# Head norms of two query stages: squares in two rounded halves, a new order on ScalarE and VectorE

## The chip, the cores and the metric

One core of a Trainium2 chip runs the whole kernel in one launch. The metric is the device time of that launch in microseconds; each kernel is executed several times, and the median counts. The core's engines run in parallel, each its own list in order, and wait for each other on semaphores: TensorE (PE: matmuls into PSUM), VectorE (DVE), ScalarE (ACT), GpSimd (POOL), and SyncE (SP), which here issues the DMAs.

## The reference

A transformer block (pooling mixer, windowed attention, convolutional FFN) is followed by two blocks with joint context: grouped-query attention, called l0, and latent attention, called l1, over 1024 tokens of width 1024 and 256 context tokens. What matters here is how queries and keys are made: project, norm each head of 64, rotate.

```python
def rms_norm(x, w):
    xf = x.astype(jnp.float32)
    y = xf * lax.rsqrt(jnp.mean(xf * xf, axis=-1, keepdims=True) + NORM_EPS)
    return (y * w.astype(jnp.float32)).astype(x.dtype)
...
    # first block
    q = partial_rope(rmsnorm(q, q_norm[l]), positions) * scale
    k = partial_rope(rmsnorm(k, k_norm[l]), positions)
...
    # second block
    k, v, q, g = jnp.split(h @ p["w_in"], cuts, axis=-1)
    q = apply_axial_rope(rms_norm(q.reshape(B, S, GQA_KV_HEADS, GQA_GROUP_2, GQA_HEAD_DIM), p["q_norm"]), cos, sin)
    k = apply_axial_rope(rms_norm(k.reshape(B, S, GQA_KV_HEADS, GQA_HEAD_DIM), p["k_norm"]), cos, sin)
```

## The kernel before

Activations lie transposed: features on the 128 partitions, tokens along the free axis. Every projection is made in split precision. Weights and inputs are each stored as a high part, rounded to fp32r, and a low part, the rounding's remainder; `split3` (L279) issues hi*hi, hi*lo and lo*hi into one PSUM bank. Weights come in panels of 128 output features by 1024: the SP queue loads a panel to `w_stage` (`load_next`, L200), ScalarE rounds it to `w_hi` (`next_hi`, L236, the instruction at L227), VectorE subtracts to `w_lo` (`next_lo`, L244, at L233). Two panel buffers alternate.

The stages in question are the first block's queries (stream q, 8 panels), and the second's queries (stream l0_q, 8 panels) and keys (stream l0_k, 2 panels). One **unit** is one panel, two heads, times one chunk of tokens. The first block has chunks of 512 and 512 (`CHUNKS_X`); l0 has 512, 512 and 256 (`CHUNKS_ALL`), called A, B and C here. That gives 16, 24 and 6 units. The work of a unit u:

- TensorE: 24 projection matmuls (8 steps of `split3`) into a bank; the stages use 4 banks, in l0 3, in turn. Then `pe_mean` (L895) of the unit **before**: the squares times a block matrix of ones, which sums them over each head. It is a plain fp32 matmul; the profile shows it as two rows of one line, L898. So the order is products(u+1), mean(u), products(u+2), mean(u+1), and at the end of a stage mean of the last but one and mean of the last unit follow each other directly (`lagged`, L917).
- ScalarE: `act_raw` (L829): Square of the bank to `heads_sq` (L833), then the bank times the gain to `heads_zg` (L834), which also sets the bank free. After the mean, `act_scale` (L859): Ln and Exp(-0.5 x) give the reciprocal root `heads_rs` (L862, L864). Its order is scale(u), raw(u+1).
- VectorE: `dve_finish` (L866): zg times cos (L882), shuffle (L884), times sin (L885), add (L886), times rs (L888), then a cast to fp32r, the high part of the query (`heads_qh`, L891), and a subtraction for the low part (`heads_ql`, L892).
- SP: stores both parts to DRAM (L910, L911).

The order of all this is written by hand, in loops that each engine runs for itself (`heads_pe`, `heads_act`, `heads_dve`, `heads_sp`); two panels make one loop body. At a stage's end the other engines wait for each other and for the stores (`end_phase`, L173), but TensorE goes on with the next stage's products as far as weights and free banks allow. Behind the keys comes the value stage (`l0_v`), whose banks are cleared by ScalarE and VectorE once they have left the key stage. The first block's keys (`kv1_*`) use the same helper class with their own calls, as do the heads of l1.

Of the kernel before, what the change touches and what calls it, by code (L numbers as in the profile page):

```python
# [104 lines left out]
def mixed_program(nc, A, out):  # L105

    ctx = ExitStack()
    with ctx:

        def sem(name):  # L110
            return ctx.enter_context(nc.semaphore(name))
# [4 lines left out]
        class Scope:  # L116


            def __init__(self):
                self.stack = ExitStack()  # L120
# [679 lines left out]
        class HeadBuffers:  # L800
            def __init__(self, name, scope):
                def two(what, dt=F32):
                    return [scope.sb(f"{name}_{what}{b}", [P, C], dt) for b in range(2)]
                self.ZG, self.SQ, self.RS = two("zg"), two("sq"), two("rs")
# [4 lines left out]
        heads_before = [0, 0]  # L809

        class Heads:

# [2 lines left out]

            def __init__(self, units, bufs, rows, dim, gain, sums, tables, mask, evacuated=None):
# [6 lines left out]
                self.j0, self.l0 = heads_before  # L825
                heads_before[0] += units
                heads_before[1] += units * self.links

# [64 lines left out]
                   .then_inc(self.split, 1)  # L893

            def pe_mean(self, pe, j, b, n):  # L895
                pe.wait_ge(self.sq, j + (self.j0 + 1))
                r = self.rows
                pe.matmul(SIDE[b][0:r, 0:n], self.sums.bitcast(F32), self.b.SQ[b][0:r, 0:n], start=True, stop=True)\  # L898
                  .then_inc(self.mean, 1)

            def begin(self, dve):
# [11 lines left out]
        def body_units(st, chunks, per_panel=1):  # L913

            return [(s, m, c, o, n) for s in range(2) for m in range(per_panel) for c, (o, n) in enumerate(chunks)]
# [14 lines left out]
                        finish(i, u - 1)  # L930
            pairs(eng, st.panels // 2, body)

        def heads_act(act, hd, st, chunks, banks, per_panel=1):
            act.preload_act_table_set(LN_EXP)
            units = body_units(st, chunks, per_panel)
            U = len(units)

            def begin(i, u):
                n = units[u][4]
                act.wait_ge(units_done, i * U + (st.u0 + u + 1))  # L940
                hd.act_raw(act, i * U + u, u % 2, BANK[u % banks][0:hd.rows, 0:n], n)


            lagged(act, st, U, begin, lambda i, u: hd.act_scale(act, i * U + u, u % 2, units[u][4]), finish_first=True,
                   after=lambda i, last, s: next_hi(act, st, i, last, s))

        def heads_dve(dve, hd, st, chunks, per_panel=1):
            units = body_units(st, chunks, per_panel)
            U = len(units)
            hd.begin(dve)  # L950

            def body(i, last):
                for u in range(U):
                    if (u + 1) % (U // 2) == 0:
                        next_lo(dve, st, i, last, 2 * u // U)
                    hd.dve_finish(dve, i * U + (EVAC_CREDIT + st.u0 + u + 1), i * U + u, u % 2, units[u][3], units[u][4],
                                  i * (U // 2) + u // 2)
            pairs(dve, st.panels // 2, body)

        def heads_pe(pe, hd, st, chunks, banks, HH, HL, kt=KT, per_panel=1, width=P, ready=None):  # L960
# [89 lines left out]
        heads_q1 = Heads(16, hb1, P, 64, vec("q_gain"), blocks[:, :], (COS1, SIN1), MASK1)  # L1050
# [1182 lines left out]
        tmp = Scope()  # L2233
        hb0 = HeadBuffers("heads0", tmp)
        MASK_GQA = [r ^ 16 for r in range(32)]
        heads_q0 = Heads(24, hb0, P, 64, vec("l0_q_gain"), blocks[:, :], TAB0, MASK_GQA)
        heads_k0 = Heads(6, hb0, P, 64, vec("l0_k_gain"), blocks[:, :], TAB0, MASK_GQA)
        tmp.close()
        tmp = Scope()
        values0 = Values("l0v", tmp, 256)  # L2240
# [1002 lines left out]
```

## Time and profile before

| what | value |
|---|---|
| median of 3 executions | 3487.97 us (3487.5 to 3494.04) |
| the profiled execution | 3487.57 us, span of its trace 3485.8 us |
| TensorE busy, share of the span | 3358.7 us, 96% |
| VectorE, ScalarE, GpSimd busy | 64%, 51%, 43% |
| first query stage in the trace | about 153 to 260 us |
| second query stage | about 1548 to 1678 us |
| keys of l0 | about 1678 to 1712 us |

The page of the profile gives busy time by engine, a chain of work that ended last (followed back from the last instruction through whatever released each), and groups of instructions. The trace below it is read by stretches of time. A row "[1.62 <-ACT heads_sq L833]" says that the engine stood idle for 1.62 us before this instruction, until that one had ended. Ends of matmuls are modelled: consecutive matmuls overlap in the rows, and the distance of their starts is what they cost.

### The profile page before, as it was taken

Reading aid. Unit: us, or ns where it says so; the run is one execution under the profiler, and the core shown is the slowest. Engines: PE = TensorE matmul, PEld = TensorE weight load, DVE = VectorE, ACT = ScalarE, POOL = GpSimd, SP = SyncE. Lnnn points to the kernel's source line nnn. Section 1 sums busy time; section 2 is a strip of 40 time slices with the busy share of each in tenths; the row PEclk is TensorE's granted clock in tenths of the full one; section 3 lists DMA queues with packets and bytes.
Section 4 is the critical chain, followed back from the end, with each engine's and each line's share of the span. In section 5 each row is a group of like instructions: output and inputs, shape, how many; then the busy total and the mean of one; then the engine's idle time right before and its main releaser. Section 6 shows DMA issues by size and latency. Waiting matters only on the chain.

```text
span 3485.8 us, 48222 instructions
## 1 busy us (share of the span) xinstructions
PE 3358.7 (96%) x15124; PEld 2675.2 (77%) x15124; DVE 2247.7 (64%) x2664; ACT 1768.6 (51%) x3036; POOL 1506.3 (43%) x952
## 2 busy tenths in 40 slices
PE   7999999999999999999999999999998999999999
PEld 5777878778888888778877777768675668888877
DVE  6674878577576665648627777767548875555551
ACT  3342868332010100234329999971455658888880
POOL 3402444444444444310037777757220026666652
PEclk9999999999999999999999999999999999999999
DMA  2134232411212121123344344323245344233312
GB/s 102 49 117 127 61 82 55 151 49 56 89 47 93 53 79 64 43 78 111 119 129 92 75 105 98 84 68 111 100 182 161 129 128 120 61 80 68 69 43 72
DMA packets 196086, 313.53 MB, mean 90 GB/s; under 512 B 100928, under 2 KB 111680, under 8 KB 195968
## 3 DMA queue, kind: packets, MB, share of 16 engines
q1 hardware_dynamic: 195968, 312.01, 31.1%
q8 instruction: 68, 1.11, 0.1%
q14 instruction: 50, 0.41, 0.0%
HBM read 234.02 MB, written 77.92 MB: 89 GB/s over the span
## 4 chain that ended last, share of the span: by engine, by line
PE 65%; POOL 10%; issue 10%; DVE 9%; ACT 4%; DMA 1%; SPq 0%; ACTq 0%; POOLq 0%; DVEq 0%
PE PBX L281 10%; PE PBX L283 10%; PE PBX L282 10%; POOL gqa_pl L2156 8%; PE PMX L281 5%; PE PMX L282 5%; PE PMX L283 5%; PE PD L2072 2%; PE PMX L2027 2%; PE PD L2073 2%; PE PD L2074 2%; PE PBX L2054 2%; PE PD L898 2%; PE PBX L2053 2%; PE PBX L2055 2%
## 5 line engine op out<-in xcount | busy, mean ns | idle before, releaser
L216 POOL TENSOR_TENSOR w_hi<-w_stage,zero 128x1024 fp32r<-128x1024 f32 (+2 forms) x123 | 227.2, 1847 | 1280.3 <-PE PBX L283 783.6
L2156 POOL TENSOR_TENSOR gqa_pl<-gqa_pf,gqa_ph 128x512 fp32r<-128x512 f32 (+1 forms) x288 | 381.7, 1342 | 138.4 <-ACT gqa_ph L2115 136.7
L2156 POOL TENSOR_TENSOR mla_pl<-mla_pf,mla_ph 128x512 fp32r<-128x512 f32 x256 | 341.2, 1338 | 190.3 <-ACT mla_ph L2115 184.8
L218 POOL TENSOR_TENSOR w_lo<-w_stage,w_hi 128x1024 fp32r<-128x1024 f32 (+2 forms) x123 | 300.4, 2442 | 9.6
L2178 DVE TENSOR_REDUCE mla_m<-PMX 128x1 f32<-128x1280 f32 x126 | 187.9, 1492 | 172.5 <-PE PMX L2027 172.5
L2178 DVE TENSOR_REDUCE gqa_m<-PMX 128x1 f32<-128x1280 f32 (+1 forms) x142 | 198.6, 1398 | 153.4 <-PE PMX L2027 152.7
L1720 ACT ACTIVATE conv_in<-PBX 128x512 f32<-128x512 f32 x66 | 39.5, 599 | 480.6 <-PE PBX L283 476.7
L2109 ACT ACTIVATE mla_pf<-PBX 128x512 f32<-128x512 f32 x320 | 190.2, 594 | 75.4 <-PE PBX L2055 61.1
L2115 ACT ACTIVATE gqa_ph<-gqa_pf 128x512 fp32r<-128x512 f32 (+1 forms) x352 | 215.0, 611 | 12.1
L2109 ACT ACTIVATE gqa_pf<-PBX 128x512 f32<-128x512 f32 (+1 forms) x352 | 200.6, 570 | 26.4 <-PE PBX L2058 20.3
L281 PE MATMUL PBX<-ffn_hi,w_hi 128*128 128x512 f32 x528 | 206.8, 392 | 3.8 <-DVE ffn_lo L672 3.8
L2115 ACT ACTIVATE mla_ph<-mla_pf 128x512 fp32r<-128x512 f32 x320 | 201.8, 631 | 11.4
L283 PE MATMUL PBX<-ffn_hi,w_lo 128*128 128x512 f32 x528 | 205.5, 389 | 0.0
L282 PE MATMUL PBX<-ffn_lo,w_hi 128*128 128x512 f32 x528 | 205.5, 389 | 0.0
L1747 DVE SCALAR_TENSOR_TENSOR conv_out<-conv_in,VEC,conv_out 128x1024 f32<-128x1024 f32 x88 | 187.0, 2125 | 12.8 <-DVE conv_out L1747 0.6
L281 PE MATMUL PBX<-l_hi,w_hi 128*128 128x512 f32 (+1 forms) x408 | 159.1, 390 | 8.1 <-DVE l_lo L672 6.2
L1743 DVE TENSOR_SCALAR conv_out<-conv_in,VEC 128x1024 f32<-128x1024 f32 x44 | 71.7, 1630 | 137.4 <-ACT conv_in L1720 137.2
L451 DVE SCALAR_TENSOR_TENSOR PMX<-mod_w,cond_s 128x1024 f32<-128x1024 f32 x96 | 151.8, 1581 | 5.7 <-DVE PMX L451 0.6
L1482 POOL TENSOR_TENSOR swa_pl<-swa_pf,swa_ph 128x512 fp32r<-128x512 f32 x64 | 81.2, 1269 | 158.9 <-ACT swa_ph L1426 158.6
L283 PE MATMUL PBX<-l_hi,w_lo 128*128 128x512 f32 (+1 forms) x408 | 146.3, 359 | 0.0
L282 PE MATMUL PBX<-l_lo,w_hi 128*128 128x512 f32 (+1 forms) x408 | 146.1, 358 | 0.0
L281 PE MATMUL PBX<-h_hi,w_hi 128*128 128x512 f32 x336 | 139.7, 416 | 6.6 <-POOL w_lo L1468 5.4
(430 smaller groups left out, 9966.2 us busy)
## 6 DMA issues: line engine op xcount, KB each, us to landing
mod_w<-in_w_mod SPq DMA_DIRECT2D x48, 512.0 KB, 3.5
w_stage<-in_w_up SPq DMA_DIRECT2D x44, 512.0 KB, 3.5
w_stage<-in_w_go SPq DMA_DIRECT2D x24, 512.0 KB, 3.6
gqa_k<-kh_d SPq DMA_DIRECT2D x32, 320.0 KB, 4.8
gqa_q<-qh_d SPq DMA_DIRECT2D x32, 320.0 KB, 6.9
w_stage<-in_w_down SPq DMA_DIRECT2D x24, 384.0 KB, 3.1
qh_d<-heads_qh SPq DMA_DIRECT2D x32, 256.0 KB, 2.1
ql_d<-heads_ql SPq DMA_DIRECT2D x32, 256.0 KB, 2.3
```

The costliest lines, as they stand in the source:

```text
L216: pool.tensor_tensor(w_hi[s][:, 0:st.cols], w_stage[s][:, 0:st.cols], z, ALU.add).then_inc(w_hi_done, 1)
L218: pool.tensor_tensor(w_lo[s][:, 0:st.cols], w_stage[s][:, 0:st.cols], w_hi[s][:, 0:st.cols].bitcast(F32), ALU.subtract).then_inc(w_split, 1)
L281: pe.matmul(ps, wh, xh, start=first, stop=False)
L282: pe.matmul(ps, wh, xl, start=False, stop=False)
L283: return pe.matmul(ps, wl, xh, start=False, stop=last)
L451: dve.scalar_tensor_tensor(out=PMX[:, C:3 * C], in0=bufs[s], scalar=1.0, in1=conds[j], op0=ALU.mult, op1=ALU.mult, accum_out=MOD[:, bass.d ...
L1482: pool.tensor_tensor(swa_PL[K % 4][:, :, 0:m], swa_PF[K % 2][:, :, 0:m], swa_PH[K % 4][:, :, 0:m].bitcast(F32), ALU.subtract).then_inc(a1[ ...
L1747: dve.scalar_tensor_tensor(out=y, in0=CU[s][:, j:j + S], scalar=w(j), in1=y, op0=ALU.mult, op1=ALU.add).then_inc(conv_step, 1)
L2109: act.activation(self.PF[k % 4][:, 0:n], self.S[k % 2][:, 0:n], ACT.Exp, scale=self.scale)\
L2115: act.activation(self.PH[k % 4][:, 0:n], self.PF[k % 4][:, 0:n], ACT.Copy).then_inc(self.hi, 1)
L2156: eng.tensor_tensor(self.PL[k % 4][:, 0:n], self.PF[k % 4][:, 0:n], self.PH[k % 4][:, 0:n].bitcast(F32), ALU.subtract).then_inc(self.lo_dv ...
L2178: dve.tensor_reduce(self.M[g % 2][:, t:t + n], MX[:, 0:n * w].rearrange("p (n w) -> p n w", n=n), AX.X, ALU.max, negate=True).then_inc(sel ...
```

## The change

A second way to norm heads is added, used by all three stages named above (`heads_act`, `heads_dve` and `heads_pe` now issue only it). The mean is made of two fp32r matmuls in place of one fp32 matmul, and its input of two parts: ScalarE rounds the squares to a high half, VectorE subtracts to a low half. The query's high part is rounded by ScalarE in place of VectorE. VectorE works in the order rotate(u), times rs(u), [w_lo], low part(u), cos(u+1), low half of the squares(u+1); ScalarE in the order scale(u), Square(u+1), query high(u), zg(u+1), squares high(u+1), [w_hi]. The mean of a unit now waits for VectorE's low half of the squares. The new buffers `sq_low` and `sq_high` lie on the same memory as `sq` and `rs`.

```diff
+            def act_begin(self, act, j, b, ps, n):
+                act.wait_ge(self.split, j + (self.j0 + 1))
+                act.activation(self.b.SQ[b][:, 0:n], ps, ACT.Square).then_inc(self.sq, 1)
+            def act_halves(self, act, j, b, ps, n):
+                act.activation(self.b.ZG[b][:, 0:n], ps, ACT.Copy, scale=self.gain).then_inc(self.evacuated, 1)
+                act.wait_ge(self.sq, j * 2 + (self.s0 + 1))
+                act.activation(self.b.RSR[b][:, 0:n], self.b.SQ[b][:, 0:n], ACT.Copy).then_inc(self.sq, 1)
+            def act_high(self, act, j, b, n, pair):
+                act.wait_ge(self.link, j * self.links + (self.l0 + 5))
+                act.wait_ge(self.stored[b], pair * 32 + (16 * self.j0 + 32))
+                act.activation(self.b.QH[b][:, 0:n], self.b.T1[:, 0:n], ACT.Copy).then_inc(self.link, 1)
+            def dve_squares_low(self, dve, j, b, n):
+                dve.wait_ge(self.sq, j * 2 + (self.s0 + 2))
+                sq = self.b.SQ[b][:, 0:n]
+                dve.tensor_tensor(self.b.SQR[b][:, 0:n], sq, self.b.RSR[b][:, 0:n].bitcast(F32), ALU.subtract).then_inc(squares_split, 1)
...
+            def dve_low(self, dve, j, b, n, pair):
+                dve.wait_ge(self.link, j * self.links + (self.l0 + 6))
+                dve.wait_ge(self.stored[b], pair * 32 + (16 * self.j0 + 32))
+                dve.tensor_tensor(self.b.QL[b][:, 0:n], self.b.T1[:, 0:n], self.b.QH[b][:, 0:n].bitcast(F32), ALU.subtract)\
+                   .then_inc(self.split, 1)
+            def pe_mean_halves(self, pe, j, b, n):
+                pe.wait_ge(squares_split, j + (self.p0 + 1))
+                pe.matmul(SIDE[b][:, 0:n], self.sums, self.b.RSR[b][:, 0:n], start=True, stop=False)
+                pe.matmul(SIDE[b][:, 0:n], self.sums, self.b.SQR[b][:, 0:n], start=False, stop=True)\
+                  .then_inc(self.mean, 1)
...
-            lagged(pe, st, U, products, lambda i, u: hd.pe_mean(pe, i * U + u, u % 2, units[u][4]))
+            lagged(pe, st, U, products, lambda i, u: hd.pe_mean_halves(pe, i * U + u, u % 2, units[u][4]))
```

VectorE in the key stage of l0, from the low part of unit A to the low part of unit C. Before:

```order
L892 TENSOR_TENSOR heads_ql<-heads_t,heads_qh 128x512
L882 TENSOR_TENSOR heads_t<-heads_zg,l_table 128x512
L884 STREAM_SHUFFLE heads_zs<-heads_zg 128x512
L885 TENSOR_TENSOR heads_zs<-heads_zs,l_table 128x512
L886 TENSOR_TENSOR heads_t<-heads_t,heads_zs 128x512
L888 TENSOR_TENSOR heads_t<-heads_t,heads_rs 128x512
L891 CAST heads_qh<-heads_t 128x512
L892 TENSOR_TENSOR heads_ql<-heads_t,heads_qh 128x512
L233 TENSOR_TENSOR w_lo<-w_stage,w_hi 128x1024
L882 TENSOR_TENSOR heads_t<-heads_zg,l_table 128x256
```

Now, from the low part of A on (L953) to the low part of C:

```order
L953 TENSOR_TENSOR heads_ql<-heads_t,heads_qh 128x512
L932 TENSOR_TENSOR heads_t<-heads_zg,l_table 128x256
L927 TENSOR_TENSOR heads_sq_low<-heads_sq,heads_sq_high 128x256
L938 STREAM_SHUFFLE heads_zs<-heads_zg 128x256
L940 TENSOR_TENSOR heads_zs<-heads_zs,l_table 128x256
L942 TENSOR_TENSOR heads_t<-heads_t,heads_zs 128x256
L948 TENSOR_TENSOR heads_t<-heads_t,heads_rs 128x256
L233 TENSOR_TENSOR w_lo<-w_stage,w_hi 128x1024
L953 TENSOR_TENSOR heads_ql<-heads_t,heads_qh 128x256
```

The cast (L891) has left VectorE, the squares' low half (L927) of the next unit stands behind its cos product, and w_lo has moved behind the product with rs of the panel's last unit.

ScalarE at the same place, from Ln of unit A to the panel's w_hi. Before:

```order
L862 ACTIVATE heads_rs<-PD 128x512
L864 ACTIVATE heads_rs<-heads_rs 128x512
L833 ACTIVATE heads_sq<-PBX 128x512
L834 ACTIVATE heads_zg<-PBX,VEC 128x512
L862 ACTIVATE heads_rs<-PD 128x512
L864 ACTIVATE heads_rs<-heads_rs 128x512
L833 ACTIVATE heads_sq<-PBX 128x256
L834 ACTIVATE heads_zg<-PBX,VEC 128x256
L227 ACTIVATE w_hi<-w_stage 128x1024
```

Now, from Ln of unit B, which is the same place but for one unit:

```order
L869 ACTIVATE heads_rs<-PD 128x512
L871 ACTIVATE heads_rs<-heads_rs 128x512
L912 ACTIVATE heads_sq<-PBX 128x256
L922 ACTIVATE heads_qh<-heads_t 128x512
L915 ACTIVATE heads_zg<-PBX,VEC 128x256
L917 ACTIVATE heads_sq_high<-heads_sq 128x256
L227 ACTIVATE w_hi<-w_stage 128x1024
```

Two instructions per unit are added to ScalarE. The first of them (L922) waits for VectorE's product with rs, and zg and the squares' high half are queued behind it.

TensorE at the end of the key stage, now:

```order
L283 MATMUL PBX<-l_hi,w_lo 128x256
L958 MATMUL PD<-heads_sq_high,blocks 128x512
L959 MATMUL PD<-heads_sq_low,blocks 128x512
L958 MATMUL PD<-heads_sq_high,blocks 128x256
L959 MATMUL PD<-heads_sq_low,blocks 128x256
```

The four matmuls of the last two means stand where two plain ones stood, behind the same narrow products of unit C.

## Rows read from the trace of the kernel before

**Rows 1.** the page's chain that ended last, share by engine

```profile
PE 65%; POOL 10%; issue 10%; DVE 9%; ACT 4%; DMA 1%; SPq 0%; ACTq 0%; POOLq 0%; DVEq 0%
```

**Rows 2.** query stages: stretch, us, busy of PE, PEld, DVE, ACT, POOL; granted clock

```profile
153.00:260.00 107.00, 104.69 (x420) 78.34 (x418) 75.98 (x127) 45.48 (x73) 4.29 (x2) 1.00 0.30 108
1548.00:1678.00 130.00, 128.23 (x624) 103.96 (x624) 97.50 (x188) 55.93 (x104) 4.29 (x2) 1.00 0.31 108
```

**Rows 3.** timeline, first query stage: start, us, engine, line, operation, tiles

```profile
178.28 1.02 PE L898 MATMUL PD<-heads_sq,blocks 128*128 128x512 f32 x2
...
179.34 0.60 ACT L862 ACTIVATE heads_rs<-PD 128x512 f32<-128x512 f32 x1 [4.13 <-PE PD L898]
179.38 0.39 PE L282 MATMUL PBX<-h_lo,w_hi 128*128 128x512 f32 x1
...
179.97 0.63 ACT L864 ACTIVATE heads_rs<-heads_rs 128x512 f32<-128x512 f32 x1
...
180.51 0.58 ACT L833 ACTIVATE heads_sq<-PMX 128x512 f32<-128x512 f32 x1
...
180.64 0.69 DVE L888 TENSOR_TENSOR heads_t<-heads_t,heads_rs 128x512 f32<-128x512 f32 x1 [1.75 <-ACT heads_rs L864]
...
180.99 0.68 ACT L834 ACTIVATE heads_zg<-PMX,VEC 128x512 f32<-128x512 f32 x1
...
181.48 0.43 DVE L891 CAST heads_qh<-heads_t 128x512 fp32r<-128x512 f32 x1
...
181.94 0.69 DVE L892 TENSOR_TENSOR heads_ql<-heads_t,heads_qh 128x512 fp32r<-128x512 f32 x1
...
182.65 1.22 DVE L233 TENSOR_TENSOR w_lo<-w_stage,w_hi 128x1024 fp32r<-128x1024 f32 x1
...
183.79 0.68 DVE L882 TENSOR_TENSOR heads_t<-heads_zg,cos 128x512 f32<-128x512 f32 x1
...
184.40 0.72 DVE L884 STREAM_SHUFFLE heads_zs<-heads_zg 128x512 f32<-128x512 f32 x1
...
184.74 1.02 PE L898 MATMUL PD<-heads_sq,blocks 128*128 128x512 f32 x2
185.16 0.69 DVE L885 TENSOR_TENSOR heads_zs<-heads_zs,sin 128x512 f32<-128x512 f32 x1
```

**Rows 4.** timeline, second query stage: the means of C, A and B

```profile
1601.20 0.59 PE L898 MATMUL PD<-heads_sq,blocks 128*128 128x256 f32 x2
...
1607.13 1.02 PE L898 MATMUL PD<-heads_sq,blocks 128*128 128x512 f32 x2
...
1610.85 1.02 PE L898 MATMUL PD<-heads_sq,blocks 128*128 128x512 f32 x2
```

**Rows 5.** costliest groups of the page: a copy to fp32r on ScalarE

```profile
L2115 ACT ACTIVATE mla_ph<-mla_pf 128x512 fp32r<-128x512 f32 x320 | 201.8, 631 | 11.4
```

**Rows 6.** timeline, end of the first query stage

```profile
258.66 1.13 PE L898 MATMUL PD<-heads_sq,blocks 128*128 128x512 f32 x2 [1.83 <-ACT heads_sq L833]
...
261.14 0.63 PE L281 MATMUL PBX<-h_hi,w_hi 128*128 128x512 f32 x1
...
261.56 0.63 PE L282 MATMUL PBX<-h_lo,w_hi 128*128 128x512 f32 x1
```

**Rows 7.** timeline, ends of second query stage and keys, value stage behind

```profile
1677.49 0.70 PE L898 MATMUL PD<-heads_sq,blocks 128*128 128x256 f32 x2 [1.62 <-ACT heads_sq L833]
...
1711.81 0.70 PE L898 MATMUL PD<-heads_sq,blocks 128*128 128x256 f32 x2 [1.62 <-ACT heads_sq L833]
...
1723.68 0.39 PE L281 MATMUL PBX<-w_hi,l_hi 128*128 128x256 f32 x1 [0.61 <-DVE l0v_lo L1033]
```

**Rows 8.** busy us by engine, granted clock (after POOL): two idle stretches

```profile
256.70:260.30 3.60, 1.50 (x4) 0.58 (x4) 2.10 (x5) 3.41 (x6) 0.00 (x0) 1.00 0.00 0
260.30:263.60 3.30, 3.30 (x9) 2.58 (x9) 3.23 (x6) 0.95 (x2) 0.00 (x0) 0.52 0.42 159
...
2612.00:2636.00 24.00, 15.63 (x59) 8.80 (x57) 23.03 (x34) 12.69 (x24) 0.00 (x0) 1.00 0.58 208
```

More of the change, by code:

```diff
@@ L803, in two @@
                     return [scope.sb(f"{name}_{what}{b}", [P, C], dt) for b in range(2)]
-                self.ZG, self.SQ, self.RS = two("zg"), two("sq"), two("rs")
+                self.ZG = two("zg")
+                inner = Scope()
+                self.SQ, self.RS = [[inner.sb(f"{name}_{what}{b}", [P, C]) for b in range(2)] for what in ("sq", "rs")]
+                inner.close()
+                self.SQR, self.RSR = two("sq_low", R32), two("sq_high", R32)
                 self.QH, self.QL = two("qh", R32), two("ql", R32)
@@ L808, in mixed_program, with __init__ @@
         head_sems = [sem(f"heads_{x}") for x in ("squares", "mean", "rsqrt", "link", "split", "stored0", "stored1")]
-        heads_before = [0, 0]
+        squares_split = sem("heads_squares_split")
+        heads_before = [0, 0, 0, 0]
         class Heads:
-            def __init__(self, units, bufs, rows, dim, gain, sums, tables, mask, evacuated=None):
+            def __init__(self, units, bufs, rows, dim, gain, sums, tables, mask, evacuated=None, split_squares=False):
                 self.evacuated = unit_evac if evacuated is None else evacuated
@@ L823, in __init__ @@
                 (self.sq, self.mean, self.rs, self.link, self.split, *self.stored) = head_sems
-                self.j0, self.l0 = heads_before
+                self.j0, self.l0, self.s0, self.p0 = heads_before
+                heads_before[2] += units * (2 if split_squares else 1)
+                heads_before[3] += units if split_squares else 0
                 heads_before[0] += units
@@ new lines, in dve_rotate @@
+            def dve_rotate(self, dve, j, b, o, n):
+                zs, t1 = self.b.ZS[:, 0:n], self.b.T1[:, 0:n]
+                at = self.l0 + 1
+                dve.stream_shuffle(zs, self.b.ZG[b][:, 0:n], self.mask).then_inc(self.link, 1)
+                dve.wait_ge(self.link, j * self.links + (at + 1))
+                dve.tensor_tensor(zs, zs, self.tables[1][:, o:o + n], ALU.mult).then_inc(self.link, 1)
+                dve.wait_ge(self.link, j * self.links + (at + 2))
+                dve.tensor_tensor(t1, t1, zs, ALU.add).then_inc(self.link, 1)
+                dve.wait_ge(self.link, j * self.links + (at + 3))
@@ L931, in lagged, with heads_act @@
             pairs(eng, st.panels // 2, body)
-        def heads_act(act, hd, st, chunks, banks, per_panel=1):
+        def heads_act(act, hd, st, chunks, banks):
             act.preload_act_table_set(LN_EXP)
-            units = body_units(st, chunks, per_panel)
+            units = body_units(st, chunks)
             U = len(units)
             def begin(i, u):
-                n = units[u][4]
                 act.wait_ge(units_done, i * U + (st.u0 + u + 1))
-                hd.act_raw(act, i * U + u, u % 2, BANK[u % banks][0:hd.rows, 0:n], n)
-            lagged(act, st, U, begin, lambda i, u: hd.act_scale(act, i * U + u, u % 2, units[u][4]), finish_first=True,
-                   after=lambda i, last, s: next_hi(act, st, i, last, s))
@@ L947, in heads_dve, with halves, body @@
-        def heads_dve(dve, hd, st, chunks, per_panel=1):
-            units = body_units(st, chunks, per_panel)
+                hd.act_begin(act, i * U + u, u % 2, BANK[u % banks][:, 0:units[u][4]], units[u][4])
+            def halves(i, u):
+                hd.act_halves(act, i * U + u, u % 2, BANK[u % banks][:, 0:units[u][4]], units[u][4])
+            begin(0, 0)
+            halves(0, 0)
+            def body(i, last):
+                for u in range(U):
+                    n, more = units[u][4], u + 1 < U or not last
+                    hd.act_scale(act, i * U + u, u % 2, n)
+                    if more:
+                        begin(i + (u + 1) // U, (u + 1) % U)
+                    hd.act_high(act, i * U + u, u % 2, n, i * (U // 2) + u // 2)
+                    if more:
+                        halves(i + (u + 1) // U, (u + 1) % U)
+                    if u + 1 < U and (u + 2) % (U // 2) == 0:
+                        next_hi(act, st, i, last, 2 * (u + 1) // U)
@@ L949, in heads_dve, with cos, squares @@
+            pairs(act, st.panels // 2, body)
+        def heads_dve(dve, hd, st, chunks):
+            units = body_units(st, chunks)
             U = len(units)
             hd.begin(dve)
+            def cos(i, u):
+                hd.dve_cos(dve, i * U + (EVAC_CREDIT + st.u0 + u + 1), i * U + u, u % 2, units[u][3], units[u][4])
+            def squares(i, u):
+                hd.dve_squares_low(dve, i * U + u, u % 2, units[u][4])
+            cos(0, 0)
+            squares(0, 0)
             def body(i, last):
@@ L958, in heads_dve @@
+                    if u + 1 < U or not last:
+                        cos(i + (u + 1) // U, (u + 1) % U)
+                        squares(i + (u + 1) // U, (u + 1) % U)
             pairs(dve, st.panels // 2, body)
```

23 lines of the change are left out of this document (17 added, 6 removed).

## The prediction

> **What bounds the kernel now.** I read the chain that ended last first: TensorE carries 65% of it, no other engine more than 10% [rows 1]. The reader is to see that a microsecond in a query stage counts only if TensorE is later or earlier for it. Then the busy times by stage: in the first query stage TensorE is busy 104.69 of 107.00 us, in the second 128.23 of 130.00, VectorE 71% and 75%, ScalarE 43% [rows 2]. So both stages run at TensorE's pace, and the others have room on average. The timeline then says what TensorE does and who follows whom. In the first query stage one unit (24 projection matmuls, then the mean of the previous unit) takes 184.74 - 178.28 = 6.46 us [rows 3]. In the second a panel has chunks of 512, 512 and 256 columns. Call them A, B, C. Means of C and A start 5.93 us apart, those of A and B only 3.72, since only the 24 narrow matmuls of C lie between [rows 4]. That short step will matter. TensorE has no wait inside the loops, only at the stage ends [rows 6, 7].
>
> **The mean itself: a gain on TensorE.** From the start of the mean to the second ordinary matmul behind it takes 179.38 - 178.28 = 1.10 us [rows 3]. An ordinary 512-wide matmul takes (6.46 - 0.87) / 24 = 0.233, where 0.87 is what the old mean adds: 1.10 less one step of 0.233. The two new matmuls are of the ordinary kind, 0.47 together. Gain 0.40 us. There are 36 such units (16 in the first stage; 16 and 4 in the second stage's queries and its keys, which go through the same functions), 14.4 us; for the ten 256-wide units I take half, 0.20 each, 2.0. Together **-16.4 us** of TensorE work. Its input, however, is now last in a longer chain.
>
> **The new chain from mean to mean.** T is the start of unit u's mean, for 512 columns. Old: Ln starts T + 1.06, Exp 0.63 later, and the next Square 0.54 behind Exp; that Square was all that the next mean needed (about T + 2.8) [rows 3]. New:
> - the second matmul starts T + 0.23 and lasts 0.39, so Ln starts at T + 0.66 (the rows leave 0.04 from a matmul's or Exp's end to who waits for it: 179.30 to 179.34, 180.60 to 180.64); Exp ends T + 0.66 + 0.63 + 0.63 = T + 1.92;
> - VectorE multiplies t by rs, 0.69: T + 1.96 to 2.65 [rows 3];
> - ScalarE rounds the query, behind the Square: a 512-wide copy to fp32r takes 0.63 [rows 5]: T + 2.69 to 3.32. It replaces VectorE's cast of 0.43, and crosses two engines. Behind it zg and the squares' high half follow at steps of about 0.55 and 0.57, the latter ending about T + 4.45;
> - VectorE's query low half T + 3.36, then cos 0.72 later, then the squares' low half 0.62 later (steps as 181.94 to 182.65 and 183.79 to 184.40 [rows 3]), which takes 0.69: T + 5.39. The mean can start at **T + 5.43**.
>
> VectorE loses the cast and gains a 0.69 subtraction per unit, 0.26 net; of 75% busy this is covered. The buffers' reuse adds no wait: the mean of a unit is read before Ln overwrites its high half.
>
> **First query stage.** TensorE reaches its next mean at T + 0.47 + 5.59 = T + 6.06. The chain is ready at 5.43: covered by 0.6. In every second unit VectorE also makes w_lo before the low half, a step of 1.14 [rows 3]: multiply 1.96, w_lo 2.68, low 3.82, cos 4.54, squares' low 5.16 to 5.85: ready at T + 5.89, covered by less than 0.2. The rotation behind it (shuffle 0.76, multiply and add about 0.73 each) then ends about 0.1 after Exp, which the next unit's slack takes up. So the 6.4 us of this stage are kept, on a thin margin. If register waits make that step 0.3 dearer, 8 units lose 0.1 each.
>
> The panel split is also later, past the next rotation: its hi part on ScalarE keeps its place, its lo part lands 4 us later, but is wanted only one unit after that; the SP queue reloads the stage buffer from the next loop body on, behind stores that were issued after the split before as well. I cost it at nothing.
>
> **Second query stage and keys.** After A's mean TensorE has 0.46 + 24 narrow matmuls, 3.72 - 0.87 = 2.85, so it stands at T + 3.31 and the squares of B are ready at T + 5.43: it waits **2.1 us**, where it waited for nothing. No later step gives this back, since the next mean is bound by TensorE again (24 wide matmuls, 5.93 less some 0.45 for the narrow mean, are 5.5 [rows 4], against 5.1 for the chain). It happens once a panel, 8 + 2 panels: **+21 us**. Against about 1.0 saved in a panel, the panel gets 1.1 us longer.
>
> **Stage ends.** The last two means stand back to back, so nothing covers the chain. Before, TensorE waited 1.83 us in the first stage [rows 6], 1.62 in the second and 1.62 in the keys [rows 7]. After, the first ends with T + 5.43 - 0.47 = 4.96, +3.1. In the others the rotation of B starts only when its squares are done, at about T - 0.1, so multiply by rs starts T + 2.14, query high 2.87 to 3.50, low 3.54, cos of C 4.26, its squares' low 4.60 to 5.02, mean T + 5.06: a wait of 4.6, +3.0 each. Behind the keys TensorE stood another 0.61 at 1723.68 for the value stage's evacuation, which starts once the key stores have landed [rows 7]; those come no later, so that wait goes: +2.4 there. Together **+8.5 us**.
>
> **Clock.** Around the first stage's end TensorE was busy 1.50 of 3.60 us, and from 260.3 to 263.6 the granted clock was 0.52, that is 1.2 GHz for nearly all of it, with matmuls 0.42 apart [rows 6, 8]. That costs half of 3.3 us, 1.7. At the two other ends a 2.1 us wait, one short mean and a 4.6 us wait now stand together, emptier than that stretch, so I charge 1.7 at each: **+3.4**; the first end pays already. For the ten waits of 2.1 us alone I charge nothing: between 2612 and 2636 TensorE was busy 15.63 of 24 us in short waits and kept 1.00 [rows 8].
>
> **Sum.** -16.4 + 21 + 8.5 + 3.4 = +16.5 us. The profiled execution took 3487.57 (span 3485.8 and 1.8 around it), 0.4 below the median: **3504 us**. The chain's unknowns: both copies at a Square's 0.58 [rows 3] take 0.1 off each of 13 waits, four handovers 0.05 dearer add 0.2: -1 to +3. The clock's: 0 to 3.3 at each end. So the forecast's own range is 3498 to 3511.
>
> **Rivals.**
> - *The clock falls inside the loops too.* A panel would then have an idle stretch of 2.1 us within some 6 us, about as empty locally as the one that cost the clock at 257 (1.50 of 3.60 us busy). Each fall costs up to 1.7 us: three of ten give 3509, all ten 3521. For it: the single wait is longer than any in the stretch that held 1.00. Against: 5.5 us of dense matmuls before and after. The Trainium skill, "TensorE: Matmul & The Clock Gate", section "A second HAM failure mode: psum-queue depth-cycling", says that idling often between groups of matmuls makes the clock swing and costs throughput; by that rule the larger figure would be the likelier, whereas the stretch from 2612 to 2636 does not agree.
> - *The wait is shorter than summed*: if ScalarE's copies took only the cast's 0.43 and two handovers overlapped, a wait of 1.3 in place of 2.1 and 3.8 in place of 4.6, without a clock loss at the ends: 16.5 - 13 x 0.8 - 3.4 = +3, 3490.
> - *The chain is covered altogether, and it is faster.* It would have to fit in the 3.3 us that C's narrow matmuls give, 2.1 less than the rows sum to. Then only the ends' waits would be left beside the 16.4 saved: about 3480; with those gone too, 3471. The deciding point is a chain of 3.3 us; Ln, Exp, the multiply and two copies are 3.2 by themselves, so I see no way but records that overstate latency.
> - *The pair of matmuls saves nothing*, if each costs a switch of kind as the old mean did: 16.5 + 16.4, 3521. Against it, matmuls of this kind follow each other at 0.233 all through the stage.
>
> **Chances.** Forecast 0.60, clock in the loops 0.19, shorter wait 0.13, covered 0.05, pair saves nothing 0.03. What a measurement of this kernel can tell from no change is about 0.2%, 7 us: faster (under 3481) 0.05, same 0.13, slower (over 3495) 0.82. The range of 8 in 10 leaves out the covered case, half of the short wait and the extreme of the clock: 3493 to 3519.
>
> **What the profile of the changed kernel would show.** The mean as two rows about 0.23 apart and Ln 0.66 after the first; in the first stage units of 6.06 us and no wait of TensorE; in the second a wait of about 2.1 us before the mean of each second chunk, on VectorE's squares low, and means of A and B 5.4 apart; waits of 4.6 to 5 at three ends; 1.2 GHz behind the ends and not inside the loops. It would be wrong if the waits in the loop were under 1 us, if the first stage's units stayed over 6.2, or if the clock fell in the loops.

## The result, and the profile of the changed kernel

| | kernel before | changed kernel |
|---|---|---|
| time, us | 3487.77 median of 4 (3487.5 to 3494.04) | 3513.8 median of 4 (3509.91 to 3515.75) |
| ratio to before | | 1.0069, 95% interval 1.0056 to 1.0082 |
| profiled execution, us | 3487.57, span 3485.8 | 3515.26, span 3513.5 |
| mean granted clock | 0.991 | 0.986 |

The change costs 26 us: slower, as forecast, and 10 us above the predicted 3504. The measured 3513.8 lies above the forecast's own range (3498 to 3511) and inside the range of 8 in 10 (3493 to 3519). The profiled executions are 27.7 us apart.

The list of waits says at once where TensorE stands (line waited at, releaser: us in total, times, longest). First the changed kernel:

```profile
PE PD L958 <- DVE heads_sq_low L927: 34.2, 13, 4.9
```

Thirteen waits, all on the low half of the squares: ten in loops and three at ends. A timeline of the second stage shows one of the ten, with the chain from the mean of A to that of B, the answer to [rows 4]:

```profile
1608.07 0.39 PE L958 MATMUL PD<-heads_sq_high,blocks 128*128 128x512 f32 x1
1608.30 0.40 PE L959 MATMUL PD<-heads_sq_low,blocks 128*128 128x512 f32 x1
1608.73 0.60 ACT L869 ACTIVATE heads_rs<-PD 128x512 f32<-128x512 f32 x1 [3.00 <-PE PD L959]
1609.36 0.63 ACT L871 ACTIVATE heads_rs<-heads_rs 128x512 f32<-128x512 f32 x1
...
1610.03 0.69 DVE L948 TENSOR_TENSOR heads_t<-heads_t,heads_rs 128x512 f32<-128x512 f32 x1 [1.03 <-ACT heads_rs L871]
1610.76 0.63 ACT L922 ACTIVATE heads_qh<-heads_t 128x512 fp32r<-128x512 f32 x1 [0.27 <-DVE heads_t L948]
...
1611.42 0.69 DVE L953 TENSOR_TENSOR heads_ql<-heads_t,heads_qh 128x512 fp32r<-128x512 f32 x1 [0.70 <-ACT heads_qh L922]
...
1612.15 0.69 DVE L932 TENSOR_TENSOR heads_t<-heads_zg,l_table 128x512 f32<-128x512 f32 x1
1612.76 0.68 DVE L927 TENSOR_TENSOR heads_sq_low<-heads_sq,heads_sq_high 128x512 fp32r<-128x512 f32 x1
...
1613.50 0.50 PE L958 MATMUL PD<-heads_sq_high,blocks 128*128 128x512 f32 x1 [1.93 <-DVE heads_sq_low L927]
1613.84 0.40 PE L959 MATMUL PD<-heads_sq_low,blocks 128*128 128x512 f32 x1
```

Read it downwards: Ln at T + 0.66, the multiply at T + 1.96, the query's high half at 2.69, its low half at 3.35, cos at 4.08, the squares' low half at 4.69, the mean of B at T + 5.43. Each link is where the forecast put it. In the first stage nothing waits, and units are 184.07 - 177.99 = 6.08 us apart where they were 6.46 [rows 3]:

```profile
177.99 0.40 PE L958 MATMUL PD<-heads_sq_high,blocks 128*128 128x512 f32 x1
...
184.07 0.40 PE L958 MATMUL PD<-heads_sq_high,blocks 128*128 128x512 f32 x1
```

The ends of the three stages, the answers to [rows 6, 7]:

```profile
256.51 0.79 PE L958 MATMUL PD<-heads_sq_high,blocks 128*128 128x512 f32 x1 [4.93 <-DVE heads_sq_low L927]
...
1687.79 0.58 PE L958 MATMUL PD<-heads_sq_high,blocks 128*128 128x256 f32 x1 [4.40 <-DVE heads_sq_low L927]
...
1732.09 0.58 PE L958 MATMUL PD<-heads_sq_high,blocks 128*128 128x256 f32 x1 [4.40 <-DVE heads_sq_low L927]
```

And the clock, in the windows view of the changed kernel (stretch, its length, busy us of PE, PEld, DVE, ACT, POOL, then granted clock): the loop of the second stage, its end's wait and what follows, a loop wait of the keys, and the keys' end.

```profile
1561.00:1683.00 122.00, 107.05 (x548) 90.77 (x548) 94.22 (x179) 70.05 (x133) 0.00 (x0) 1.00 0.29 104
1684.20:1687.80 3.60, 0.01 (x1) 0.01 (x1) 2.71 (x7) 3.01 (x6) 0.00 (x0) 0.50 0.01 5
1687.80:1694.40 6.60, 6.34 (x15) 4.90 (x16) 3.04 (x6) 1.86 (x4) 0.00 (x0) 0.50 0.32 116
1694.40:1700.00 5.60, 5.60 (x26) 4.57 (x26) 1.39 (x4) 2.34 (x4) 0.00 (x0) 1.00 0.50 189
1708.10:1711.50 3.40, 3.40 (x8) 2.72 (x9) 2.62 (x4) 1.62 (x4) 0.00 (x0) 0.50 0.22 84
...
1732.10:1738.80 6.70, 6.44 (x28) 6.17 (x29) 3.04 (x6) 1.22 (x3) 0.00 (x0) 0.50 0.33 117
```

The seven loop waits between 1561 and 1683 leave the clock at 1.00, 2.4 GHz. Each of the two ends loses it: within its wait the clock is at 0.50, 1.2 GHz, which costs nothing there, and stays for 6.6 and 6.7 us of dense work behind, which costs up to half of that, **3.3 us per end**. The same ends before held 1.00 (before, the two ends):

```profile
1679.20:1689.40 10.20, 10.20 (x46) 8.45 (x45) 5.01 (x12) 2.73 (x4) 0.00 (x0) 1.00 0.35 115
1710.20:1713.60 3.40, 1.53 (x9) 1.16 (x10) 3.26 (x7) 3.31 (x7) 0.00 (x0) 1.00 0.41 154
```

**The 27.7 us by stage.** The projection matmuls at the start of the second stage and behind its queries, its keys and its values are the same instructions in both kernels, so the difference of their starts is what has been lost so far. Before:

```profile
1548.15 0.47 PE L281 MATMUL PBX<-l_hi,w_hi 128*128 128x512 f32 x1 [0.26 <-issue]
...
1678.46 0.47 PE L281 MATMUL PBX<-l_hi,w_hi 128*128 128x512 f32 x1 [0.27 <-issue]
...
1712.77 0.36 PE L281 MATMUL PBX<-w_hi,l_hi 128*128 128x256 f32 x1 [0.26 <-issue]
...
1744.02 0.47 PE L281 MATMUL PBX<-l_hi,w_hi 128*128 128x512 f32 x1 [1.36 <-DVE l0v_lo L1033]
```

After:

```profile
1545.13 0.47 PE L281 MATMUL PBX<-l_hi,w_hi 128*128 128x512 f32 x1 [0.26 <-issue]
...
1688.85 0.76 PE L281 MATMUL PBX<-l_hi,w_hi 128*128 128x512 f32 x1 [0.26 <-issue]
...
1733.15 0.55 PE L281 MATMUL PBX<-w_hi,l_hi 128*128 128x256 f32 x1 [0.26 <-issue]
...
1766.04 0.47 PE L281 MATMUL PBX<-l_hi,w_hi 128*128 128x512 f32 x1 [1.38 <-DVE l0v_lo L1122]
```

| stretch | forecast by its terms | measured |
|---|---|---|
| up to the second stage | -6.4 + 3.1 = -3.3 | -3.0 |
| its queries | -8.0 + 16.8 + 3.0 = +11.8 | +13.4 |
| its keys | -2.0 + 4.2 + 3.0 + 1.7 = +6.9 | +10.0 |
| its values | -0.6 + 1.7 = +1.1 | +1.6 |
| all behind, unchanged code | 0 | +5.7 |
| sum | +16.5 | +27.7 |

### The profile page after: what moved, and what is told of

Same layout as the page of the kernel before. It is cut to its first block, busy times and chain, and to the rows that moved or that the text cites. A ratio compares the mean times of both kernels' runs of the same rounds, so it can differ in the third digit from the quotient of the medians.

```text
span 3513.5 us, 48417 instructions
## 1 busy us (share of the span) xinstructions
PE 3355.3 (95%) x15124; PEld 2682.1 (76%) x15124; DVE 2254.6 (64%) x2664; ACT 1819.3 (52%) x3128; POOL 1507.5 (43%) x952
## 4 chain that ended last, share of the span: by engine, by line
PE 65%; POOL 11%; DVE 10%; issue 9%; ACT 5%; DMA 0%; ACTq 0%; DVEq 0%; POOLq 0%; SPq 0%
PE PBX L281 10%; PE PBX L282 10%; PE PBX L283 10%; POOL gqa_pl L2245 9%; PE PMX L281 5%; PE PMX L282 5%; PE PMX L283 5%; PE PD L2161 2%; PE PMX L2116 2%; PE PD L2162 2%; PE PD L2163 2%; PE PBX L2143 2%; PE PBX L2142 2%; PE PBX L2144 2%; PE PD L905 1%
## 5 line engine op out<-in xcount | busy, mean ns | idle before, releaser
L2161 PE MATMUL PD<-gqa_ph,gqa_v 128*128 128x512 f32 x320 | 137.9, 431 | 7.7 <-POOL gqa_pl L2245 4.3
```

The lines of the kernel that those rows point to most:

```text
L2161: pe.matmul(o, self.V[q][0][:, t, :], ph, start=first, stop=False)
```

## The experiments

All kernels were compared with runs of the kernel before on the same chip, whose medians there were 3489.96, 3489.99, 3491.47 and 3491.65 us; so ratios, not times, are compared across groups; the microseconds given with a ratio are that share of the kernel before (by its ratio the change itself costs 24 us, by its medians 26). "The shift" is the difference of the same instruction's start to the kernel before.

**1 and 2. One stage alone.** The flag `split_squares` chooses between the old and the new functions. In first_only it is taken from `heads_q0` (and from `heads_k0` alike), in second_only from `heads_q1`:

```diff
-        heads_q0 = Heads(24, hb0, P, 64, vec("l0_q_gain"), blocks[:, :], TAB0, MASK_GQA, split_squares=True)
+        heads_q0 = Heads(24, hb0, P, 64, vec("l0_q_gain"), blocks[:, :], TAB0, MASK_GQA)
```

> Only the first query stage works in the new way, the l0 queries and keys as before. Theory (the gain is kept where 24 wide matmuls cover the chain, and the loss is in l0): units of 6.08 us in the first stage as in the changed kernel, one wait of about 5 us at its end, and the work behind it 3 us earlier than before: 3482 to 3487 us, about 3 under before. Rival (the new order as such costs, on every stage): slower than before.

> Only the l0 queries and keys work in the new way, the first stage as before. Theory: all of the loss is here, about 10 waits of 2.0 us, two end waits of 4.4, and half clock behind the ends: 3487.8 + 25 to 31, so 3512 to 3519, as slow as the changed kernel or slower. Rival: about half of the loss, 3500.

first_only: 3488.35 us, ratio 0.9995 (0.9985 to 1.0004), above my 3482 to 3487, and no change that can be told. second_only: 3517.53 us, ratio 1.0075 (1.0058 to 1.0091), as expected. 0.9995 x 1.0075 = 1.0070, the 1.0069 of both: the whole loss is in the second stage and its keys. The first stage's 3 us show in its profile (a shift of -2.9 us at 1545), but at the end of that execution it stands at +3.3: the code behind, which is untouched, lost them again and more.

**3. The squares first.** The suspect is the place of the squares at the end of the chain. Here they are made and rounded on ScalarE ahead of Ln, and VectorE subtracts ahead of the multiply by rs. The amount of work is unchanged. In short form, the body of the loop of each engine:

```diff
-act_scale(u); begin(u + 1); act_high(u); zg(u + 1); squares_high(u + 1)
+begin(u + 1); squares_high(u + 1); act_scale(u); zg(u + 1); act_high(u)
-rotate(u); scaled(u); w_lo; low(u); cos(u + 1); squares(u + 1)
+rotate(u); squares(u + 1); scaled(u); w_lo; low(u); cos(u + 1)
```

> The changed kernel, but the next unit's squares are made ready before the present unit is scaled: ScalarE in the order Square(u+1), its high half, Ln(u), Exp(u), zg(u+1), query high(u); VectorE makes the squares' low half before the product with rs. The work is the same. Theory (TensorE waits for the length of the chain from mean to mean, not for anybody's load): the squares are ready at about T + 2.2 instead of T + 5.4, under the 3.3 us of the narrow step, so the ten waits of 2 us and the 4.4 to 5 us at the ends go, and with them the half clock: the 16.4 us of TensorE work come back, less up to 6 us where VectorE's serial chain (5.7 us per wide unit, plus w_lo) gets later than TensorE in l0: 3471 to 3480 us. Rival (ScalarE's and VectorE's added instructions load them too much): 3500 and more, with waits of the same size.

3485.2 us, ratio 0.9988 (0.9978 to 0.9998). From 1.0069 that is 28 us. Means and an end of the second stage in its timeline:

```profile
1660.10 0.39 PE L960 MATMUL PD<-heads_sq_high,blocks 128*128 128x512 f32 x1
...
1664.09 0.50 PE L960 MATMUL PD<-heads_sq_high,blocks 128*128 128x512 f32 x1 [0.49 <-DVE heads_sq_low L929]
...
1669.43 0.58 PE L960 MATMUL PD<-heads_sq_high,blocks 128*128 128x256 f32 x1 [4.61 <-DVE heads_sq_low L929]
```

Six loop waits of 0.3 to 0.5 us are left of the ten of 2.0, and the first stage's end waits 2.05 us where it waited 4.93, so the order made them, as the forecast's chain says. But the wait at the end of the queries stays at 4.61, that of the keys at 4.58, and the time misses my 3471 to 3480. VectorE explains it:

```profile
1665.33 0.69 DVE L955 TENSOR_TENSOR heads_ql<-heads_t,heads_qh 128x512 fp32r<-128x512 f32 x1 [0.70 <-ACT heads_qh L924]
...
1666.12 0.69 DVE L934 TENSOR_TENSOR heads_t<-heads_zg,l_table 128x512 f32<-128x512 f32 x1
...
1666.53 0.42 ACT L916 ACTIVATE heads_sq_high<-heads_sq 128x256 fp32r<-128x256 f32 x1
...
1666.74 0.72 DVE L940 STREAM_SHUFFLE heads_zs<-heads_zg 128x512 f32<-128x512 f32 x1
...
1667.50 0.69 DVE L942 TENSOR_TENSOR heads_zs<-heads_zs,l_table 128x512 f32<-128x512 f32 x1
...
1668.22 0.69 DVE L944 TENSOR_TENSOR heads_t<-heads_t,heads_zs 128x512 f32<-128x512 f32 x1
...
1668.95 0.42 DVE L929 TENSOR_TENSOR heads_sq_low<-heads_sq,heads_sq_high 128x256 fp32r<-128x256 f32 x1
```

The high half of C's squares was ready at 1666.53 + 0.42 = 1666.95. VectorE, which had been idle for 0.70 us until ScalarE's cast had ended, ran the whole rotation of B ahead of the subtraction, which started only at 1668.95. It was the later engine.

**4. The cast back on VectorE.** The query's high half is made by VectorE, as before; all else as in the changed kernel.

```diff
-                act.activation(self.b.QH[b][:, 0:n], self.b.T1[:, 0:n], ACT.Copy).then_inc(self.link, 1)
+                dve.tensor_copy(self.b.QH[b][:, 0:n], self.b.T1[:, 0:n]).then_inc(self.link, 1)
```

> The changed kernel, but the query's high part is again a cast on VectorE, right before the low part. Theory: the chain loses the crossing to ScalarE (0.63 and two handovers) and gains the cast (0.43 to 0.46), so each of the 13 waits is 0.2 to 0.3 us shorter, 3 us in all, and the waits stay: 3507 to 3512 us. Rival (the crossing to ScalarE is what makes TensorE wait): the waits fall under 1 us and the time under 3500.

3509.88 us, ratio 1.0054 (1.0037 to 1.0071), inside the range expected, though the interval overlaps the changed kernel's. The thirteen waits are together 2.9 us shorter:

```profile
PE PD L958 <- DVE heads_sq_low L927: 31.3, 13, 4.7
```

So ScalarE's cast, with its two handovers, is about 0.2 us of each 2.1: a small part.

**5. The pair alone.** The kernel before, with the mean taken by two matmuls over the same rounded squares. The low half is left out.

```diff
-                pe.matmul(SIDE[b][0:r, 0:n], self.sums.bitcast(F32), self.b.SQ[b][0:r, 0:n], start=True, stop=True)\
...
+                pe.matmul(SIDE[b][:, 0:n], self.sums, self.b.SQ[b][:, 0:n], start=True, stop=False)
+                pe.matmul(SIDE[b][:, 0:n], self.sums, self.b.SQ[b][:, 0:n], start=False, stop=True)\
+                      .then_inc(self.mean, 1)
```

> The kernel before, where the mean of the three stages is taken by two matmuls over the same rounded squares (ScalarE writes the squares rounded, Ln's scale is halved) in place of the one matmul in full float32. The low half is left out: nothing is added on ScalarE or VectorE and no wait is added. My theory: the 36 wide means and 10 narrow ones save 0.40 and 0.20 us each, 16.4 us in all, and all of it shows, as TensorE bounds these stages: 3470 to 3476 us against 3488, with the query stages' units 5.6 us apart where they were 6.06. Rival (the pair saves nothing, or VectorE's 4.8 us per unit and ScalarE take over): 3484 to 3490 us.

3478.25 us, ratio 0.9961 (0.9946 to 0.9975): 13.6 us faster, 2 us above my range. (The 5.6 and 6.06 us between units in that expectation were a slip for 6.06 and 6.46; measured were 6.08.) In its profile the shift moves by -6.1 us over the first stage, to -4.6 at 1545. The matmuls behind the queries and behind the keys, at 1678.46 and 1712.77 before, are here:

```profile
1665.49 0.76 PE L281 MATMUL PBX<-l_hi,w_hi 128*128 128x512 f32 x1 [0.26 <-issue]
...
1699.35 0.37 PE L281 MATMUL PBX<-w_hi,l_hi 128*128 128x256 f32 x1 [0.26 <-issue]
```

So the shift is -13.0 and then -13.4: the queries save 8.4 us where 8.0 were forecast, the keys only 0.4 of 2.0. Between them the clock fell behind the queries' end (a row of this is shown in the last section), and from the last mean of the queries to the first of the keys 13.34 us pass where 11.95 did, with a mean that is 0.2 cheaper: 1.6 us. Together 14.9 us show, and 16.5 with that loss set aside, for the 16.4 of the forecast's first term. Behind the keys 0.7 us are given back in the value stage and another 2.2 before 1845. The rival that the pair saves nothing falls. That a change of the kind of matmul costs anything, as that rival assumes of the old mean, no run shows.

**6. The clock kept at the ends.** The changed kernel, with matmuls of ones in the waits:

```diff
+                if isinstance(i, int) and i == final and u == U - 1:
+                    keep_clock(pe, BANK[5], 17)
                 hd.pe_mean_halves(pe, i * U + u, u % 2, units[u][4])
```

> The changed kernel, where TensorE fills its wait ahead of the last mean of each of the three stages with 17 matmuls of ones (17 x 0.23 = 3.9 us, into a bank that is free, read by nobody). My theory: the two ends of the second query stage and of the keys cost, beside their waits of 4.4 us, the 10 us at half clock that follow each: with the clock kept the run is 8 to 11 us shorter than the changed kernel, 3503 to 3506 us, the waits shown there fall to about 0.5 us, and the granted clock over 1690 to 1735 is 0.95 or more where it was 0.84. Rival (the clock behind the ends costs no time, since other engines bound what follows, the 26 us lie in the waits): 3511 to 3516 us.

3509.29 us, ratio 1.0046 (1.0029 to 1.0063): less than the changed kernel's by 0.0023, 8 us, but the intervals overlap. The windows show what happened (two loop waits, then the two ends):

```profile
1562.00:1565.40 3.40, 2.89 (x7) 2.31 (x8) 2.83 (x6) 1.50 (x3) 0.00 (x0) 0.54 0.41 154
1599.50:1602.90 3.40, 3.40 (x11) 2.65 (x10) 2.51 (x5) 2.77 (x7) 0.00 (x0) 0.55 0.02 7
1680.00:1700.00 20.00, 17.15 (x85) 14.04 (x84) 11.93 (x22) 11.06 (x20) 0.00 (x0) 1.00 0.25 86
1725.00:1745.00 20.00, 17.12 (x122) 15.59 (x121) 10.21 (x21) 7.47 (x15) 0.00 (x0) 1.00 0.40 139
```

The ends hold 1.00, but in this execution these two loop waits lost the clock, which had kept it in the changed kernel. The time alone settles nothing; the stages do:

| stage | shift gained, changed kernel, us | shift gained, clock_kept_at_ends, us |
|---|---|---|
| queries, with the two falls | +13.4 | +16.2 |
| keys, behind the queries' end | +10.0 | +7.1 |
| values, behind the keys' end | +1.6 | -0.8 |
| from there to 1845 | +0.9 | +2.4 |

Behind the two ends 5.3 us are won, of the 6.6 that two times 3.3 would be; 2.8 of it went in the loop, where two falls cost up to 1.7 each, and 1.5 behind the values. (The 10 us at half clock in that expectation count the part inside the wait too; behind it are 6.6.)

**7. The same on squares_first.**

> squares_first (3485 us) with the 17 matmuls of ones ahead of the last mean of each of the three stages. My theory: its waits of 4.6 us at the ends of the second query stage and of the keys are each followed by 6.8 us at half clock; kept, that is 3.4 us each, so 3476 to 3481 us. Rival (the clock there costs nothing): 3484 to 3487 us. If the run comes out at 3485 though the clock stays high behind the ends, the gain was lost at other falls of the clock further on.

3487.42 us, ratio 0.9991 (0.9981 to 1.0001), no better than squares_first; the rival, at first sight. But its profile separates two things. Over the keys and the values the shift goes from -4.2 to -3.4 us, against -8.0 to -2.8 in squares_first: 4.4 us won where the clock is kept, of 6.4 at most (6.7 and 6.1 us at half clock behind the two waits). Ahead of that, at the end of the first stage, TensorE waited only 2.05 us in squares_first, and 17 matmuls of 3.9 us made it late (a shift of -5.8 us behind that end against -7.4). So in both pairs of profiles the clock behind these two ends costs time, 5.3 and 4.4 us, somewhat less than the 6.6 and 6.4 that half of the slow stretches would be; and filling a wait with more than its length costs the excess.

**8. VectorE's gap filled.** On squares_first, the shuffle of the next unit stands in the 0.7 us that VectorE idles, and the subtraction one step earlier (short form, VectorE's loop):

```diff
-rotate(u); squares(u + 1); scaled(u); w_lo; low(u); cos(u + 1)
+sin(u); squares(u + 1); add(u); scaled(u); shuffle(u + 1); w_lo; low(u); cos(u + 1)
```

> squares_first (3485 us), where VectorE's seven operations of a unit stand in another order: the next unit's shuffle fills the 0.7 us in which VectorE waits for ScalarE's cast, and the low half of the squares is taken right behind the multiplication by the sines, one operation earlier (VectorE's wait for the evacuated unit is taken by an increment of a semaphore ahead of the shuffle). My theory: what is late at a unit's mean is VectorE's chain, so its period for a wide unit falls from 6.2 to about 5.5 us, the loop waits of 0.3 to 0.5 us go and the end waits fall from 4.6 to 2 to 3.3 us: 3470 to 3480 us. Rival (ScalarE's or the stores' chain bounds, not VectorE's order): 3483 to 3487 us, as squares_first.

3482.67 us, ratio 0.9976 (0.9967 to 0.9986), 8.4 us under the kernel before and 2.7 above my range. The interval overlaps that of squares_first (0.9978 to 0.9998), so it is the waits that decide. Where nine stood, 13.8 us together:

```profile
PE PD L967 <- DVE heads_sq_low L931: 7.6, 3, 2.8
```

The loop waits are gone, and the two ends that waited 4.6 us wait 2.79: VectorE's order was the bound of squares_first, and the rival (ScalarE or the stores) falls.

**9 and 10. ScalarE's gate removed, then the clock kept.** In shuffle_ahead ScalarE's Square of C waited for the low half of A's query; its buffers are free by ScalarE's own order. Where the next unit is the narrow one, VectorE also takes its squares' low half ahead of `dve_sin`. The last line is in no_gate_clock_kept alone, at the last mean of the second stage and of the keys.

```diff
             def act_begin(self, act, j, b, ps, n):
-                act.wait_ge(self.split, j + (self.j0 + 1))
...
+                    narrow = more and units[following[1]][4] < n
+                    if narrow:
+                        squares(*following)
                     hd.dve_sin(dve, j, u % 2, o, n)
-                    if more:
+                    if more and not narrow:
                         squares(*following)
...
+                    keep_clock(pe, BANK[5], 8)
```

> shuffle_ahead (3483 us), where ScalarE's square of a unit no longer waits for VectorE's low half of the query two units back (ScalarE's own cast of that unit has already waited for the last reader of the buffers that it writes), and VectorE takes the low half of a narrow unit's squares ahead of the multiplication by the sines. My theory: the end waits of 2.8 us were this gate and VectorE's order: they fall to 1.6 to 2.3 us, and the time to 3477 to 3483 us. Rival (nothing of the 2.8 us can go, the time is set by the clock that the end of each stage loses): 3481 to 3486 us.

> no_gate with 8 matmuls of ones (8 x 0.23 = 1.9 us, into a bank that is free, read by nobody) ahead of the last mean of the second query stage and of the keys. My theory: the wait there shrinks to under 0.5 us and no half clock follows, which gives back 1.7 to 3.4 us at each end: 3 to 6 us less than no_gate, 3472 to 3478 us. Rival (the clock falls elsewhere instead, as it did in the loop in clock_kept_at_ends, so nothing is won): within 1.5 us of no_gate.

no_gate: 3476.98 us, ratio 0.9958 (0.9944 to 0.9971), an interval that overlaps shuffle_ahead's. no_gate_clock_kept: **3475.13 us, ratio 0.9951 (0.9938 to 0.9965)**, 16.5 us under the kernel before on that chip. The end of the second stage, in the first and in the second:

```profile
1663.83 0.38 PE L966 MATMUL PD<-heads_sq_high,blocks 128*128 128x256 f32 x1 [2.07 <-DVE heads_sq_low L930]
```

```profile
1661.75 0.38 PE L966 MATMUL PD<-heads_sq_high,blocks 128*128 128x256 f32 x1 [0.22 <-DVE heads_sq_low L930]
```

The wait fell by 2.79 - 2.07 = 0.72 us, one step of VectorE, which is what the narrow subtraction moved forward. The gate alone can have held little there: in shuffle_ahead the high half of C's squares was ready at 1660.99, 0.17 us after VectorE had room for it at that earlier place (1660.82). The two edits were not run apart.

The clock there is 0.51 in the first (3.4 us behind the wait) and 1.00 in the second:

```profile
1664.30:1667.70 3.40, 3.14 (x9) 2.49 (x8) 2.94 (x7) 1.84 (x3) 0.00 (x0) 0.51 0.20 74
```

```profile
1658.00:1668.00 10.00, 9.52 (x47) 7.63 (x46) 9.37 (x18) 6.41 (x13) 0.00 (x0) 1.00 0.28 105
```

The matmuls of ones won 1.85 us in the medians, under what these intervals can tell and short of the 3 to 6 expected; the windows allow 1.7 per end. In the profiles the keys gained 0.7 us by them and the values nothing. Both kernels beat the kernel before and the changed one, with the same arithmetic as the changed one.

## Why the forecast was right in sign and short in size

- **The first term held.** The pair of matmuls saves what was forecast: 14.9 us show in pair_alone and 16.5 with its clock loss set aside, for 16.4, and the first stage's units are 6.08 us for 6.06.
- **The chain held to a hundredth** in three of the eight panels: A to B 5.43 or 5.44. In the others it was 5.56 to 5.63, 5.54 on average over all, 0.1 more; and behind a wait the second half of a mean starts 0.34 us after the first (1613.50 and 1613.84) where it is 0.23 otherwise (1608.07 and 1608.30), another 0.1. Ten waits so cost 2.0 us more than +21. One wait a panel, at the place forecast, and squares_first shows that the squares' place in the order is their cause.
- **The ends** were +3.1, +2.8 and +2.8 (waits 4.93, 4.40, 4.40) for +3.1, +3.0 and +3.0: right. At the values, TensorE's 0.61 [rows 7] went, as forecast.
- **The step that failed is the size of the clock's term.** The mechanism and its places were right: 1.2 GHz behind both ends and, nearly, none in the loops. The forecast charged 1.7 us at each end, half of the 3.3 us that the first stage's end showed [rows 8]. The wait there was 1.83; here the clock stayed down for 6.6 and 6.7 us of work behind waits of 4.40, up to 3.3 us each. With one fall in the keys' loop (1708.1, another 1.7), the clock cost up to 8.3 where 3.4 stood: 4.9 of the 11 us. The keys' excess of 3.1 in the table is 1.6 and 1.7 of it; of the second end's 3.3 the values passed on about 1.1 less than all, so not all of a slow stretch was paid. The waits in the loops add 2.0 to it and the ends take 0.4 off; what is left is the next point.
- **The unchanged code behind was charged nothing, and cost 5.7 us.** Nothing there was touched. Nearly the same 100 us of instructions, before and after, in windows shifted by 26 us:

```profile
2500.00:2600.00 100.00, 94.98 (x422) 72.31 (x421) 40.44 (x65) 54.96 (x98) 21.27 (x10) 1.00 0.39 140
```

```profile
2526.00:2626.00 100.00, 94.98 (x408) 71.72 (x407) 39.33 (x63) 53.09 (x92) 18.45 (x9) 0.97 0.38 134
```

Busy alike, clock 0.97 for 1.00. Added up, the clock stood at half for 17.1 us behind 1845 before, and for 27.3 after: half the difference, 5.1, is nearly the 4.8 lost there; 0.9 more was lost between the values and 1845. This stretch is the same code in all kernels of this study, and its loss roughly follows the clock, not the edit (pair_alone, with the same 17.1 us, differs by 1.6):

| kernel | half clock behind 1845, us | shift gained behind 1845, us |
|---|---|---|
| before | 17.1 | 0 |
| pair_alone | 17.1 | -1.6 |
| clock_kept_at_ends | 23.9 | +2.1 |
| squares_first_clock_kept | 23.9 | +1.9 |
| changed kernel | 27.3 | +4.8 |
| cast_on_vector | 27.3 | +4.6 |
| first_only | 30.7 | +5.0 |
| shuffle_ahead | 30.7 | +5.4 |
| no_gate_clock_kept | 30.7 | +6.6 |
| squares_first | 30.7 | +6.8 |
| no_gate | 34.1 | +7.1 |
| second_only | 34.1 | +7.3 |

Most of it comes from one place: between 2470 and 2600 the last eight kernels of the table lose 3.3 to 4.4 us, and the three above them nothing. The profiled execution of the kernel before was one with few falls there. It is 2 to 4 us under its medians on the other chips, though three of its four executions on its own chip lie within 0.5 us of each other. One kernel alone also varies: the kernel before took from 3484.76 us, at a mean clock of 0.993, to 3495.8, at 0.990, in its executions on the chips of this study. So chance has a part in these falls. Whether a kernel's timing has one too, one profile of each can't tell: open.

**The rivals.** The clock in the loops, at a chance of 0.19, was partly true, and with it one of the forecast's own signs of being wrong: one of ten waits lost it here, one in cast_on_vector, two in second_only, three in clock_kept_at_ends. The measured 3513.8 lies in that rival's 3509 to 3521, but only 1.7 us of the excess came from its mechanism. The row from 1561 to 1683 has seven waits of 2 us and a clock of 1.00. The Trainium skill, "TensorE: Matmul & The Clock Gate", section "A second HAM failure mode: psum-queue depth-cycling", says that frequent idling between groups of matmuls makes the clock swing. That agrees with the one to three falls of each profile, and not with the other waits. The shorter wait, the covered chain and the pair that saves nothing fell: waits 1.93 to 2.14, and 14.9 us saved in the profile of the pair.

## What to carry to other kernels

Work that is split over two engines for a cheaper matmul costs by its place in the consumer's chain, not by its amount: by the ratios, the same instructions gave +24 us with the squares' low half last, -4 us with it ahead of the scaling, and -15 us with the next unit's shuffle in VectorE's gap as well, the narrow subtraction one step earlier and a needless gate removed. Find the shortest distance between two consumers (here 3.72 us between the means of A and B, against 6.46 in the other stage) and test the chain against that one. A wait at a stage's end can be charged twice, once as itself and once for the slower clock behind it. How long that lasts can't be read from the wait: 4.3 us behind the wait of 4.93 at the first stage's end, 6.6 behind 4.40, 4.0 behind the 4.20 of cast_on_vector, 6.3 and 3.4 behind the two of 2.79 in shuffle_ahead.

## What the hardware did that was not expected

- **Equal waits, unequal clock.** Before the change the ends of the second stage and the keys waited 1.62 us and kept 1.00. pair_alone has the same two waits, of 1.62 us, and lost the clock at both (end of its second stage):

```profile
1664.72 0.38 PE L901 MATMUL PD<-heads_sq,blocks 128*128 128x256 f32 x1 [1.62 <-ACT heads_sq L835]
...
1664.90:1668.30 3.40, 3.14 (x9) 2.38 (x10) 3.26 (x6) 1.77 (x4) 0.00 (x0) 0.58 0.12 45
```

- So also for the 2 us waits in the loops: of ten in each profile, one to three lost it. A fall behind a short wait can't be forecast from the wait alone; behind waits of 2.8 us and more in these stages it came every time.
- **Half clock inside a wait is free.** Of about 10 us at 1.2 GHz at an end, 3.6 lay in the wait; only the rest is paid, at up to half of its length.
